# Sixty-four tokens fetched by index, and part of the blocks multiplied in full fp32 from their raw slots

## What is computed

```python
def peer(x, w_q, sub_keys, u, v):
    q = (xt @ w_q).reshape(T, 8, 2, 128)
    s = einsum('thpd,pnd->thpn', q, sub_keys)          # 128 sub-keys a side
    sv, si = top_k(s, 16)
    cv, ci = top_k(all 16 x 16 sums of the two sides, 16)
    experts = i1 * 128 + i2                            # (256 tokens, 128 experts each)
    gates = softmax(cv)
    a = gelu(einsum('td,tkd->tk', x, u[experts]), exact) * gates
    return einsum('tk,tkd->td', a, v[experts])
```

## Time and profile before

| | us |
|---|---|
| median of 3 runs | 1717.34 (1716.94 to 1717.40) |
| the profiled execution | 1716.15 |
| its span in the trace | 1714.3 |
| PE busy | 1689.3 (99%) |
| DVE busy | 1456.4 (85%) |
| ACT busy | 923.7 (54%) |
| POOL busy | 459.5 (27%) |
| moved by DMA | 392.28 MB, mean 229 GB/s |

### The profile page before, as it was taken

One profiled execution on the slowest core, in us unless ns is written; L12 is line 12 of the kernel. 1 busy time (PEld: TensorE's weight loads), 2 busy tenths in 40 slices (PEclk: granted clock), 3 DMA queues, 4 the chain that ended last, 5 costly groups with the idle time before them and its releaser, 6 DMA issues.

```text
span 1714.3 us, 30335 instructions
## 1 busy us (share of the span) xinstructions
PE 1689.3 (99%) x11590; PEld 1584.9 (92%) x11590; DVE 1456.4 (85%) x2651; ACT 923.7 (54%) x1497; POOL 459.5 (27%) x262
## 2 busy tenths in 40 slices
PE   8999999999999999999999999999999999999998
PEld 8888999999999999999888899999999999999996
DVE  6984899989998998889756669999899888888995
ACT  5554554656555555555535455456555555555552
POOL 6730651000001443444003018210000034434530
PEclk9999999999999999999999999999999999999999
DMA  7545556555557899899723246475555588888991
GB/s 252 191 138 185 174 183 224 183 185 185 191 190 259 312 329 340 309 328 363 284 103 123 89 158 222 157 237 175 191 189 185 196 303 327 331 315 319 346 333 48
DMA packets 108497, 392.28 MB, mean 229 GB/s; under 512 B 12353, under 2 KB 12993, under 8 KB 108097
## 3 DMA queue, kind: packets, MB, share of 16 engines
q1 hardware_dynamic: 85248, 307.42, 52.3%
q0 software_dynamic: 19072, 68.23, 10.5%
q10 hardware_dynamic: 4032, 14.68, 2.5%
HBM read 388.12 MB, written 1.05 MB: 227 GB/s over the span
## 4 chain that ended last, share of the span: by engine, by line
PE 76%; DVE 15%; DMA 4%; issue 2%; ACT 1%; SPq 0%; DVEq 0%; ACTq 0%
PE work L636 17%; PE y L755 9%; PE work L639 9%; PE work L755 9%; PE work L678 6%; PE work L760 5%; PE y L760 5%; PE y L746 4%; DMA raw<-v 4%; DVE y L1898 3%; PE y L1062 3%; PE work L696 3%; PE y L724 2%; DVE far_homes L542 2%; PE work L699 1%
## 5 line engine op out<-in xcount | busy, mean ns | idle before, releaser
L542 DVE TENSOR_TENSOR low<-raw,high 128x1024 fp32r<-128x1024 f32 x404 | 497.2, 1233 | 72.2 <-ACT high L1126 68.8
L1126 ACT ACTIVATE high<-raw 128x1024 fp32r<-128x1024 f32 x442 | 464.6, 1052 | 165.8 <-PE work L678 70.6
L636 PE MATMUL work<-xT,high 128*128 128x448 f32 x1408 | 321.7, 370 | 0.9 <-DVE low L542 0.9
L599 POOL DMA_INDIRECT big<-u_rows,picks x64 | 117.5, 1837 | 663.1 <-DVE big L1798 649.3
L636 PEld LDWEIGHTS work<-xT,high 128*128 128x128 f32 x1408 | 251.6, 189 | 18.4 <-DVE low L542 1.2
L1392 ACT ACTIVATE xT<-big 128x224 fp32r<-128x224 f32 x256 | 97.6, 387 | 214.7 <-PE work L760 213.4
L639 PEld LDWEIGHTS work<-xT,low 128*128 128x128 f32 x1408 | 184.0, 191 | 5.5
L678 PE MATMUL work<-xT,high 128*128 128x224 f32 (+1 forms) x1056 | 182.5, 277 | 3.9 <-POOL low L542 2.1
L1126 ACT ACTIVATE far_homes<-raw 128x1024 fp32r<-128x1024 f32 x138 | 144.8, 1055 | 74.4 <-DMA raw<-v 36.3
L639 PE MATMUL work<-xT,low 128*128 128x224 f32 x1408 | 184.0, 273 | 0.0
L599 POOL DMA_INDIRECT big<-v,picks x64 | 133.2, 2082 | 160.2 <-DVE big L1812 131.1
(11 more groups left out here) (243 smaller groups left out, 2942.9 us busy)
## 6 DMA issues: line engine op xcount, KB each, us to landing
raw<-u SPq DMA_DIRECT2D x256, 512.0 KB, 3.3
raw<-v SPq DMA_DIRECT2D x256, 512.0 KB, 5.4
raw<-wq SPq DMA_DIRECT2D x32, 512.0 KB, 3.2
raw<-conv_in SPq DMA_DIRECT2D x14, 512.0 KB, 4.2
aux<-ln_par ACTq DMA_DIRECT2D x9, 512.0 KB, 5.5
raw<-conv_out SPq DMA_DIRECT2D x8, 512.0 KB, 3.3
raw<-mla_out SPq DMA_DIRECT2D x8, 512.0 KB, 4.4
big<-diag ACTq DMA_DIRECT2D x6, 512.0 KB, 4.4
```

The source lines that it names most:

```text
L542: ops.tensor_tensor(low_at(c), raw[:, slot, :], high_at(c).bitcast(F32), ALU.subtract).then_inc(low_made[slot], 1)
L599: nc.gpsimd.indirect_dma_start(out=side_rows[before % SIDE_BUFS], out_offset=None, in_=rows, in_offset=bass.IndirectOffsetOnAxis(ap=pick_i ...
L636: nc.tensor.matmul(both, w_high[:, cols], xT[:, k, :, 0:DT], start=(k == 0), stop=False)
L1126: A(high_at(c), raw[:, slot, :], ACT.Copy).then_inc(high_made, 1)
```

## The change

The change takes more tokens out of the dense part and multiplies a part of the blocks without splitting them:

- `SIDE` 64 and `DT` 192: 2 groups of 64 partitions, so 64 gathers for u and 64 for v per layer, in 7 buffers. 26 dots move into late pairs 7 to 41 (`DOT_PAIRS`, odd pairs), 38 stay in v (11/10 block apart), the 64 sums follow about one per 1.06 block from block 47 to 113. 24 batches instead of 28.
- A block in `FULL` isn't split. PE takes it as full fp32 straight from its raw slot (`whole_products`, 8 matmuls of 192 columns, in v against `hid` itself). These are the 37 early blocks, block 127, every second late pair (22 of 45) and, in v, the blocks with n % 5 in (1, 3) from 3 to 116 (46). Its slot is free when PE has used it, and SP's load waits for that. The other blocks are split as before.
- `x_full`, the unsplit x of the dense tokens, is added up on POOL from high and low, once per layer, in the tile that later holds the columns; PE waits for it before block 0 of u.
- `EARLY` 37, `CHOSEN_AT` 34, `EXP_AT` 24; no lows within the selection; no far homes in u; far homes in v from block 83 (was 71).
- The three `w_uq` loads of layer 1 are issued by ACT behind the last highs of layer 0's v instead of at blocks 107 to 115.

```diff
-EARLY = 39
+EARLY = 37
-CHOSEN_AT = 37
-EXP_AT = 28
-PICK_LOWS = (31, 37)
-TOP_LOWS = {3 * _i: 2 + 4 * _i for _i in range(1, 8)}
+CHOSEN_AT = 34
+EXP_AT = 24
-SIDE = 32
+SETS = ((64, 2),)
+SIDE = sum(_n for _n, _ in SETS)
-SIDE_BUFS = 3
-SIDE_DOTS_AT = {2 + _d * 7 // 4: _d for _d in range(SIDE_ROWS)}
-SIDE_GELU_AT = 58
-SIDE_SUMS_AT = {60 + _d * 7 // 4: _d for _d in range(SIDE_ROWS)}
+SIDE_BUFS = 7
-DENSE = 8
-PAIR_OF = [_b if _b < DENSE else DENSE + (_b - DENSE) * 7 // 4 for _b in range(BATCHES)]
+PAIR_OF = [_b * (PAIRS - 3) // (BATCHES - 1) for _b in range(BATCHES)]
+FULL_PAIRS = range(1, PAIRS, 2)
+MERGED = PAIRS - len(FULL_PAIRS)
+EARLY_DOTS = 26
+DOT_PAIRS = {}
+for _d in range(EARLY_DOTS):
+    DOT_PAIRS.setdefault(7 + 2 * (_d * 18 // EARLY_DOTS), []).append(_d)
+V_DOTS = SIDE_ROWS - EARLY_DOTS
+SIDE_DOTS_AT = {2 + _d * 11 // 10: EARLY_DOTS + _d for _d in range(V_DOTS)}
+SIDE_GELU_AT = max(SIDE_DOTS_AT) + 3
+SIDE_STEP = (115 - SIDE_GELU_AT - 2) / SIDE_ROWS
+SIDE_SUMS_AT = {SIDE_GELU_AT + 2 + int(_d * SIDE_STEP): _d for _d in range(SIDE_ROWS)}
...
+def whole(layer, n):
+
+    late = n - EARLY
+    return n < EARLY or n == NKEYS - 1 or late // 2 in FULL_PAIRS
...
+FULL_V = [_n for _n in range(FIRST_COLUMNS, COLUMNS - LAST_COLUMNS) if _n % 5 in (1, 3)]
+FULL = {FIRST[f"u{_layer}"] + _n for _layer in range(DEPTH) for _n in range(NKEYS) if whole(_layer, _n)}
+FULL |= {FIRST[f"v{_layer}"] + _n for _layer in range(DEPTH) for _n in FULL_V}
...
-                    if c >= RAW:
-                        sp.wait_ge(high_made, c - RAW + 1)
-                        sp.wait_ge(low_made[c % RAW], c // RAW)
+                    if c in BEFORE:
+                        before = BEFORE[c]
+                        if before in FULL:
+                            sp.wait_ge(block_used, before + 1)
+                        else:
+                            sp.wait_ge(high_made, HIGHS[before])
+                            sp.wait_ge(low_made[RAW_SLOT[before]], LOWS[before])
...
+                nc.gpsimd.tensor_tensor(x_full[:], xT_high[:, :, 0:DT].bitcast(F32), xT_low[:, :, 0:DT].bitcast(F32),
+                                        ALU.add).then_inc(x_full_ok, 1)
...
+            def whole_products(c, out_):
+
+                for k in range(KD):
+                    mm = nc.tensor.matmul(out_, raw_at(c)[:, k * P:(k + 1) * P], x_full[:, k, :],
+                                          start=(k == 0), stop=(k == KD - 1))
+                mm.then_inc(block_used, 1)
...
+                if c in FULL:
+                    n = c - FIRST["v0" if c < FIRST["mla_in"] else "v1"]
+                    for k in chunks:
+                        mm = nc.tensor.matmul(columns_bank(k)[:, 0, :], raw_at(c)[:, k * P:(k + 1) * P], hid[:, n, :],
+                                              start=False, stop=False)
+                    return mm
...
-                    add_cross(layer, pair)
+                    if pair not in FULL_PAIRS:
+                        add_cross(layer, pair)
                     if pair + 1 == PAIRS:
                         a_lo(layer, 0)
                     make_low(dve, V, u0 + n + 4)
                     if b is not None:
                         gate(layer, b)
+                    for d in DOT_PAIRS.get(pair, ()):
+                        side_dot(layer, d)
                     late(layer, pair)
```

More of the change, by code:

```diff
@@ L99 @@
     _g += _n
+def whole(layer, n):
[4 more added lines that the diff above has]
+FULL |= {FIRST[f"v{_layer}"] + _n for _layer in range(DEPTH) for _n in FULL_V}
+A_RANK = [sum(_m not in FULL_V for _m in range(_n + 1)) for _n in range(NKEYS)]
+A_BLOCKS = A_RANK[-1]
 LEAD = {"wq0": 4, "mla_in": KQ + KKV + 1, "wq1": 4}
@@ L155 @@
 for _layer in range(DEPTH):
-    for _i in range(GROW_FROM, NKEYS + (LEAD["mla_in"] if _layer == 0 else 0)):
-        _k = (_i - GROW_FROM) % (len(V_FAR) + RING)
+    _late = [_i for _i in range(GROW_FROM, NKEYS + (LEAD["mla_in"] if _layer == 0 else 0)) if _i not in FULL_V]
+    for _n, _i in enumerate(_late):
+        _k = _n % (len(V_FAR) + RING)
         if _k < len(V_FAR):
@@ L176 @@
     _last[_home] = _c
+RAW_SLOT, BEFORE, LANDED, HIGHS, LOWS = {}, {}, {}, {}, {}
+_last, _loads, _lows, _highs = {}, {}, {}, 0
+for _c in range(_g):
+    _slot = min(range(RAW), key=lambda slot: _last.get(slot, slot - 2 * RAW))
+    if _slot in _last:
+        BEFORE[_c] = _last[_slot]
+    _last[_slot] = _c
+    _loads[_slot] = _loads.get(_slot, 0) + 1
+    RAW_SLOT[_c], LANDED[_c] = _slot, 16 * _loads[_slot]
+    if _c not in FULL:
+        _highs += 1
+        _lows[_slot] = _lows.get(_slot, 0) + 1
+        HIGHS[_c], LOWS[_c] = _highs, _lows[_slot]
+SLOTS = 1 + max(RAW_SLOT.values())
 def last_high(c):
@@ L216, in pair_banks, with merged_rank @@
     return slice(first, first + 2)
+def merged_rank(pair):
+    return sum(p not in FULL_PAIRS for p in range(pair + 1))
 def gated_tokens(pair):
@@ L1081, in wait_both @@
                     wait_low(c)
-                    pe.wait_ge(a_low, c + 1 - first + NKEYS * layer)
+                    if c not in FULL:
+                        pe.wait_ge(a_low, A_BLOCKS * layer + A_RANK[c - first])
                 for c in range(first, first + FIRST_COLUMNS):
@@ L1476, in _ @@
                 if layer + 1 < DEPTH:
+                    for n in range(3):
+                        mla_weights(n)
                     highs_to(FIRST["mla_in"] + 3)
```

221 lines of the change are left out of this document (113 added, 108 removed).

## The result

The changed kernel takes 1825.32 us (median of 4 runs, 1819.5 to 1828.68), the kernel before 1717.14 beside it. The ratio on record is 1.0614, 95% interval 1.0583 to 1.0644 (the quotient of these two medians, 1.063, lies inside). It is slower by 6%, where 1693 was forecast. The profiled execution took 1828.68 us with a span of 1826.9, 112.6 us more than the span before.

The account below looks back on a forecast made before the run. PE was taken to bound the kernel, with DMA next in v: 1717.3 - 58.4 of PE work + 2 x 15 for raw slots + 2 x 2 for late pairs = 1693 us, own range 1670 to 1715, 8-in-10 range 1661 to 1738.

Parts of the forecast that it names:

- The bound and the prices: Whole kernel: PE sets the time; full matmuls of 192 columns 162 ns per instruction, wide ones 180, narrow ones 110.
- rival 4: Split blocks: wide matmuls of 384 columns take 203 ns instead of 180, giving 1737 us; chance 0.06.
- Early u: Early blocks of u: full blocks at 2.60 us each; with the last block, 10.8 us less per layer.
- The selection and `x_full`: Around u's early blocks: both costed at nothing, the selection with 3 to 4 us cover, `x_full` behind 12 wq blocks.
- Late u: Late pairs of u: 249.6 us falls to 243.6, plus 2 per layer for waits; window named 243 to 248.
- Feed (a): v stage, bandwidth: 108 MB needs 397 GB/s; at 412 nothing is lost, at 359 29 us per layer.
- rival 3: v stage: a DMA ceiling of about 359 GB/s loses 29 us per layer, giving 1722 us; chance 0.12.
- Feed (b): v stage: SP's load waits for PE's use of a full block's slot; 0.69 us per five blocks, +15 per layer.
- rival 2: v stage: loads land in 6.9 us, 48 lost per layer, 1759 us; decides from about 6.05; chance 0.14.
- the chain's form: v stage: landing 5.4, high 1.05, low 1.23, handoffs 0.3, plus 4.96 of PE work: 12.94 us per five blocks.
- edit costed at nothing: Whole kernel: edits assumed hidden, such as selection, `x_full` and moved mla_weights; late pairs got +2 us per layer.
- Rival 1: v stage: the feed keeps up, loads land in 4.2 us at up to 412 GB/s, giving 1663 us; chance 0.18.

Follow-up runs that it names:

- pairs_third: Every third instead of every second late u pair full, on the kernel with two raw slots for full v blocks, no look-ahead, one of five full (1688.93 us): 1706.91 us.
- experiment 8: Changed kernel with two extra raw slots for full v blocks, five gather buffers, no look-ahead to block 116: 1697.44 us; with one of five v blocks full, 1688.93 us.
- experiment 1: Changed kernel with all but the first seven gathers per layer replaced by 8 KB loads, dots multiplied by zero (side tokens' output left out): 1725.52 us.
- experiment 12: SP's load waiting for PE swapped with the next, no look-ahead: every fourth v block full, 1720.82 us (1749.63 unswapped); two of five full, 1819.40 us.
- swap_nogrow: Changed kernel without the look-ahead (two of five v blocks full), with SP's load that waits for PE swapped with the one after it: 1819.40 us.
- experiment 2: Changed kernel with ScalarE making highs only five blocks ahead up to block 116, instead of up to nine from block 83: 1778.65 us.
- thin: The run of experiment 1: changed kernel with most gathers replaced by 8 KB loads, look-ahead kept: 1725.52 us.
- nogrow: The run of experiment 2: changed kernel without the look-ahead of the highs up to block 116: 1778.65 us, ratio 1.0353 to the kernel before.

## Why the prediction was wrong, point by point

**The bound and the prices: right.** PE's timeline of the kernel after, late u (count and duration to the start of the next kind): 32 full matmuls from 401.09 to 406.32, 163 ns each (162.5 forecast), 8 narrow ones 109 (110 forecast).

```profile
401.09 5.39 PE L689 MATMUL work<-columns,raw 128*128 128x192 f32 x32
406.32 1.06 PE L1144 MATMUL y<-aux 128*128 128x128 f16 x16
...
407.18 1.67 PE L709 MATMUL work<-xT,high 128*128 128x384 f32 x8
408.69 1.03 PE L712 MATMUL work<-xT,low 128*128 128x192 f32 x8
409.56 1.59 PE L709 MATMUL work<-xT,high 128*128 128x384 f32 x8
```

The wide ones take 189 and 179 ns here, 175 as the stage's median, for 180; rival 4 falls. Early u is 85.8 us for 33 blocks, 2.60 each, as forecast. The selection and `x_full` were covered, as costed: in layer 0 PE waits only once between the queries and the first late pair, 1.7 us, for a low.

**Late u: direction right, size off.** 249.5 us measured and 243.6 + 2 forecast, just outside of the 243 to 248 named. The two-pair period is right in the steady part; the rest is mostly short waits, 6.9 us in all, for DVE's onehots, lows and merges, 4.6 of them in the first 30 us. pairs_third shows how near DVE's chain there is to being late, though its share of 0.75 doesn't look like it. In the span all of u is 9.4 us over the forecast, both layers together.

**Feed (a), the rate: not the cause, and rival 3 falls.** Slots of their own let the same bytes come at 403 GB/s for 240 us. The page "DMA: Bandwidth & Descriptors" of the Trainium skill (Specifications) gives about 358 GB/s for one core's reads. The kernel after, at 347 to 358 with a share of 0.95, looked as if it stood at that limit. The page "HBM Reference" of the Trainium skill (Specifications (TRN2)) calls that number the share of one of two cores and gives about 425 for a core that streams alone. The trace of experiment 8, 403 held, is above the first figure and below the second; the prediction had weighed the first page alone.

**Feed (b), the raw slots: the step that failed, in its size.** The term was +15 us per layer; measured are 41.9 and 48.3. Its place is right: PE's idle stands ahead of the heirs, released by a low whose high waited for raw<-v, and the chain's form (landing + high + low + the two blocks up to the next full one) gave 12.94 us at a landing of 5.4. The landing I took, 5.4, was the median of loads in the kernel before, whose v stage moved 320 to 326 GB/s. Measured are 6.3 us from the slot's release to the high, beyond the 6.05 from which rival 2 decides, and 14.3 us for five blocks, rival 2's 14.44. Part A is 41.9 + 48.3 = 90 us instead of the 30 in the sum. Why the landing is longer: the gathers share the engines (3.8 us without them, experiment 1). The loads held up behind the waiting one go out with it, and for the second of them experiment 12 shows what that costs (8.3 us instead of 5.0); that it lengthens the heir's own landing isn't shown, for swap_nogrow, which was to test it, went the other way. With 6.3 the form gives 8.9 + 4.95 = 13.9; the last 0.4 us for five blocks stay open.

**What the prediction hadn't: part B, a term put at nothing.** The look-ahead stands in the description of the queues, but in no term of the sum, in no edit costed at nothing and in no rival. The trace of before gave little warning: ACT waits 15.8 us for raw<-v ahead of the highs in the ring, and 36.3 us ahead of those in the far homes, where the look-ahead works:

```profile
L1126 ACT ACTIVATE far_homes<-raw 128x1024 fp32r<-128x1024 f32 x138 | 144.8, 1055 | 74.4 <-DMA raw<-v 36.3 <-PE work L678 29.8 <-DMA raw<-u 5.9
```

That a look-ahead past a full block makes ACT wait for PE, with PE's next activations behind on the same engine, had not been considered. It costs 33.4 + 24.5 = 58 us by the columns, 47 by the medians (experiment 2).

The parts add up, as differences along one row of runs must. The forecast had -24.4 us for the span; measured is +112.6, so 137.0 are missing: part A 60.2, part B 57.9, the v columns without either part 5.8 (298.8 / 297.4 for 297.1 / 293.3), u 9.4, the other stages 3.7. With thin taken first 13 us move from part B to part A.

**The chances.** Rival 2 had 0.14, as a mechanism at 1759; nogrow, which is the change without part B, took 1779. The chance was too low for a chain whose one uncertain term, the landing, needed to move from 5.4 to 6.05 only, in a stage whose own rows went up to 6.9. Rival 1's 1663 was reached by no run: even thin_nogrow, with the gathers' traffic and the look-ahead gone, took 1682.

## What to carry to other kernels

When a buffer's release moves from a helper engine that runs ahead to the engine that sets the pace, the refill (landing, preparation, hand-over) closes into a chain with it. Compare it with the work up to its next user at the loaded landing time, not the quiet one, and add whatever stands behind that refill on its queue. Any look-ahead across such a buffer is then a wait for the future: before changing who frees a buffer, list every place that asks for it early. A full transfer pipe is shown by what it does with the wait removed; a busy share of 0.95 beside idle PE time proved nothing here.

## What the runs showed of the hardware

- One core's DMA queues moved 403 GB/s over 240 us, most 6-us slices at 399 to 415 (experiment 8). A busy share of 0.94 to 0.96 stood beside 347 to 358 GB/s in the changed kernel, so the share near 1 doesn't say how much more would go.
- A matmul with full fp32 inputs and 192 columns costs 2 x 163 ns, on the line between the 112 ns of 128 columns and the 216 of 256; an fp32r one with 384 columns costs 175.
- After 6 us of idle time PE was granted half its clock for the next 2.7 us; the v columns' mean was 0.95 and 0.94 in the changed kernel and 0.99 in the repaired one.
